# The state space stage of a hybrid decoder step in another order: samples first, one product per batch of log decays, new states on four row groups

## The reference, cut to what matters

```python
    cs = jnp.cumsum(dA, axis=-1)
    Lmat = jnp.exp(segsum(dA))
    CB = jnp.einsum('bclgn,bcsgn->bcgls', Cc, Bc)
    y_diag = jnp.einsum('bcgels,bcsgep->bclgep', CB[:, :, :, None] * Lmat, X)
    decay_states = jnp.exp(cs[..., -1:] - cs).transpose(0, 1, 4, 2, 3)
    states = jnp.einsum('bclgn,bclgep->bcgepn', Bc, X * decay_states[..., None])
    ...
    new_states = jnp.einsum('bgezc,bcgepn->bzgepn', decay_chunk, states)
    y_off = jnp.einsum('bclgn,bcgepn->bclgep', Cc, prev_states) * jnp.exp(cs).transpose(0, 1, 4, 2, 3)[..., None]
    y = (y_diag + y_off).reshape(b, L, H, P)
```

## Time and profile before

| what | value |
|---|---|
| time, median of 3 executions | 1319.71 us (1319.27 to 1320.49) |
| profiled execution: time, span | 1314.85 us, 1313.0 us |
| busy: TensorE, VectorE, ScalarE, GpSimd | 1251.3, 375.7, 229.4, 77.1 us |
| transferred, mean rate | 476.19 MB, 363 GB/s |
| mean granted TensorE clock | 0.984 |

### The profile page before, as it was taken

The page is one execution under the profiler, slowest core; times in us unless marked ns, Lnnn a source line. Parts: engine busy times, 40 slices in busy tenths (PEclk is TensorE's granted clock), DMA queues, the critical chain, the costliest instruction groups (busy, mean ns, idle before and its releaser), DMA issues.

```text
span 1313.0 us, 14836 instructions
## 1 busy us (share of the span) xinstructions
PE 1251.3 (95%) x5826; PEld 541.8 (41%) x5826; DVE 375.7 (29%) x737; ACT 229.4 (17%) x490; POOL 77.1 (6%) x62
## 2 busy tenths in 40 slices
PE   7999998898989999999999999999999999999997
PEld 5766666654433333333333333333333333333332
DVE  2478423543323212122221222212121222212122
ACT  2014434242211111111011011101101111111102
POOL 0000031646000000000000000000000000000000
PEclk9999998899989999999999999999999999999999
DMA  9688779129469999999999999999999999999993
GB/s 276 225 315 276 251 235 347 53 81 324 181 251 426 427 429 429 426 430 429 426 430 427 428 430 426 430 430 426 430 429 427 429 428 428 430 427 428 428 427 132
DMA packets 79581, 476.19 MB, mean 363 GB/s; under 512 B 7688, under 2 KB 41764, under 8 KB 52700
## 3 DMA queue, kind: packets, MB, share of 16 engines
q1 hardware_dynamic: 77278, 471.08, 88.1%
q0 software_dynamic: 688, 2.62, 0.5%
q10 hardware_dynamic: 1582, 2.03, 0.5%
HBM read 468.47 MB, written 7.24 MB: 362 GB/s over the span
## 4 chain that ended last, share of the span: by engine, by line
PE 70%; DMA 23%; DVE 3%; ACT 2%; issue 1%; POOL 1%; SPq 0%; ACTq 0%; DVEq 0%; POOLq 0%
DMA ring<-in_w 23%; PE ps L1991 22%; PE ps L2033 12%; PE ps L1526 9%; PE ps L1940 7%; PE ps L1809 3%; PE ps L1569 1%; PE ps L1948 1%; PE ps L1932 1%; PE ps L1924 1%; PE ps L2009 1%; PE ps L1982 1%; PE ps L1743 1%; PE ps L1545 1%; PE ps L1685 1%
## 5 line engine op out<-in xcount | busy, mean ns | idle before, releaser
L1991 PE MATMUL ps<-ring,own 128*64 128x512 f32 x1536 | 340.9, 593 | 17.1 <-DMA ring<-in_w 17.1
L1450 DVE TENSOR_SCALAR own<-ps 128x512 f32<-128x512 f32 x32 | 22.2, 692 | 649.0 <-PE ps L1991 649.0
L1991 PEld LDWEIGHTS ps<-ring,own 128*64 128x64 f32 x1536 | 108.8, 137 | 236.2 <-issue 197.5
L2033 PE MATMUL ps<-ring,own 128*64 128x512 f32 x768 | 172.7, 599 | 3.4 <-ACT own L953 3.4
L1526 PE MATMUL ps<-own,ring 128*128 128x288 f32 x512 | 131.7, 411 | 0.3 <-DMA ring<-in_w_in 0.3
L1991 PE MATMUL ps<-own 128*64 128x512 f32 x512 | 115.7, 593 | 2.0 <-DMA own<-in_w 2.0
L1526 PEld LDWEIGHTS ps<-own,ring 128*128 128x128 f32 x512 | 95.7, 191 | 30.7 <-issue 3.3
L2033 PEld LDWEIGHTS ps<-ring,own 128*64 128x64 f32 x768 | 54.7, 138 | 107.5 <-issue 104.2
L949 ACT ACTIVATE own<-own 128x512 f32<-128x512 f32 x32 | 20.2, 631 | 443.9 <-DVE own L1450 443.9
L1940 PE MATMUL ps<-own 128*128 128x512 f32 x180 | 90.0, 625 | 0.0
L959 ACT ACTIVATE own<-ps 64x512 f32<-64x512 f32 x64 | 37.9, 593 | 230.0 <-PE ps L2033 229.2
(11 more groups left out here) (337 smaller groups left out, 1051.9 us busy)
## 6 DMA issues: line engine op xcount, KB each, us to landing
ring<-in_w SPq DMA_DIRECT2D x144, 2048.0 KB, 30.6
own<-in_w SPq DMA_DIRECT2D x48, 2048.0 KB, 29.2
ring<-in_w_in SPq DMA_DIRECT2D x16, 1024.0 KB, 6.2
ring<-in_cache_win_k SPq DMA_DIRECT2D x16, 1024.0 KB, 6.8
ring<-in_cache_win_v SPq DMA_DIRECT2D x16, 1024.0 KB, 7.8
ring<-in_w_out SPq DMA_DIRECT2D x6, 1024.0 KB, 10.1
ring<-in_state_ssm SPq DMA_DIRECT2D x8, 512.0 KB, 6.8
out_ssm_sample<-ring SPq DMA_DIRECT2D x8, 512.0 KB, 4.4
```

The source lines that it names most:

```text
L1450: nc.vector.tensor_scalar(xg_o, hid[:, 0], LIMIT, None, ALU.min).then_inc(sem("glu_ready"), 1)
L1991: last = nc.tensor.matmul(ps[C * half:C * half + C, 1 + m, :], xT[:, k, C * u:C * u + C], rows[:, D * half + 512 * m:D * half + 512 * m + ...
L2033: last = nc.tensor.matmul(ps[C * half:C * half + C, 4, :], gT[:, (k % 4) * P + C * (k // 4):(k % 4) * P + C * (k // 4) + C], rows[:, 512 * ...
```

## The change

The stage is rewritten. The samples' rows (tile 2) come first, as one batch of 16 heads x 32 columns; the prompt's eight batches follow (BATCHES). The mask of the decays changes sides, so that a batch of log decays is a single product of 512 columns, in one bank. The old states' transposes and products run at the start of the stage. The new states of a group and of four sequences are one turn of four products with K=32, each on its own 32 partitions; VectorE multiplies the old state by its decay and adds the product in one operation per sequence. X of the samples is laid out as four blocks of rows for this (Xs), B is copied to them (Bn). Old states come in and go out with 512 neighbouring words per row piece in place of 128. Tile 1's square sums, scales and transposes move into the mix. The diff, cut:

```diff
+CHUNK_ORDER = (2, 0, 1)
+CHUNK_TURN = {c: i + 1 for i, c in enumerate(CHUNK_ORDER)}
+BATCHES = [(2, 0)] + [(c, hb) for c in range(2) for hb in range(4)]
+STATE_ON_ACT = (2, 4, 6, 7)
+STATE_ON_DVE = (0, 1, 3, 5)
+ROUNDS = [(0, 0), (1, 0), (0, 1), (1, 1)]
...
+                        sp.dma_start(state[:, b].rearrange("p g j n -> p g (j n)"),
+                                     a["state_ssm"][0, b].rearrange("h p n -> (h p) n").rearrange("(g p j) n -> p g (j n)", g=G, j=4)).then_inc(sem("states_in"), 16)
...
-            sp.wait_ge(sem("yo_ps"), 2)
+            for b in range(DB):
+                if b % 4 == 0:
+                    sp.wait_ge(sem("state_new"), 2 * b + 8)
+                sp.dma_start(o["ssm_sample"][b].rearrange("h p n -> (h p) n").rearrange("(g p j) n -> p g (j n)", g=G, j=4),
+                             state[:, b].rearrange("p g j n -> p g (j n)")).then_inc(sem("ssm_s_out"), 16)
+            sp.wait_ge(sem("M_ready"), len(BATCHES))
...
-                    sp.wait_ge(sem("yo_ps"), 2)
+                    sp.wait_ge(sem("yd_ps"), len(BATCHES))
...
+            decays_in(0)
+            nc.gpsimd.tensor_copy(d3(dAx[0:NS], 16), dA[0:NS, 32:48].unsqueeze(2).broadcast_to([NS, H, 16])).then_inc(sem("dAx_ready"), 1)
             for g in range(G):
                 nc.gpsimd.tensor_tensor(d3(CTm[g], NS), xbcT[:, 10 + g, SEQ:TOK].unsqueeze(1).broadcast_to([P, DB, NS]),
                                         d3(const("seq_cols"), NS), ALU.mult).then_inc(sem("CTm_ready"), 1)
-            pool.wait_ge(sem("fin_out"), 16)
-            nc.gpsimd.tensor_copy(d3(dAx[0:NS], HP), dA[0:NS, 32:48].unsqueeze(2).broadcast_to([NS, H, HP])).then_inc(sem("dAx_ready"), 1)
+            decays_in(1)
+            pool.wait_ge(sem("Bn_ready"), 1)
             for g in range(G):
-                nc.gpsimd.tensor_tensor(Bm[0:NS, g], Bn[0:NS, 2, g * N:(g + 1) * N].unsqueeze(1).broadcast_to([NS, DB, N]),
-                                        const("seq_of", NS).unsqueeze(2).broadcast_to([NS, DB, N]), ALU.mult).then_inc(sem("Bm_ready"), 1)
-
-            pool.wait_ge(sem("decayed_act"), 1)
-            pool.wait_ge(sem("stT_ps"), DB)
-            for j in range(0, 8, 2):
-                nc.gpsimd.tensor_tensor(state[:, :, j, :], state[:, :, j, :], edx[:, 8 * j:8 * j + 8].unsqueeze(2).broadcast_to([P, DB, N]),
-                                        ALU.mult).then_inc(sem("decayed"), 1)
-                if j == 0:
-                    gated(2)
-
-            pool.wait_ge(sem("fs_ps"), 8)
-            pool.wait_ge(sem("yd_out"), 3)
+                nc.gpsimd.tensor_tensor(Bm[:, g], Bn[:, 2, g * N:(g + 1) * N].unsqueeze(1).broadcast_to([P, DB, N]),
+                                        const("seq_of").unsqueeze(2).broadcast_to([P, DB, N]), ALU.mult).then_inc(sem("Bm_ready"), 1)
+            decays_in(2)
+            decayed_x(0)
+            decays_in(3)
+            decays_in(4)
+            gated(2)
+            decays_in(5)
+            pool.wait_ge(sem("yo_ps"), 1)
+            decayed_x(1)
+            decays_in(6)
+            decays_in(7)
+            gated(0)
+            decays_in(8)
+            gated(1)
+
+            pool.wait_ge(sem("st_ps"), 2)
...
+            chunk_decays(2)
+            chunk_decays(0)
+            act.wait_ge(sem("decay_ps"), 1)
+            nc.scalar.activation(edx, ps[:, 7, 256:272], ACT.Exp).then_inc(sem("decayed_act"), 1)
+            decay_weights(0)
+            state_columns(2)
+            state_columns(4)
+            decay_weights(1)
+            state_columns(6)
+            decay_weights(2)
+            state_columns(7)
+            decay_weights(3)
+            decay_weights(4)
+            chunk_sums(2)
+            chunk_decays(1)
+            for batch in range(5, 9):
+                decay_weights(batch)
+            chunk_sums(0)
+            act.wait_ge(sem("y_sums"), 4)
+            nc.scalar.activation(dts[:, 6:9], stat[:, 6:9], ACT.Sqrt)
+            for c in (0, 2):
+                n = ROWS[c]
+                last = nc.scalar.activation(dts[0:n, 2 * c:2 * c + 2], stat[0:n, 2 * c:2 * c + 2], ACT.Sqrt, bias=stat[0:n, 60:61])
+            last.then_inc(sem("mix_rt"), 1)
+            act.wait_ge(sem("fin_ps"), 1)
+            nc.scalar.activation(d3(fin_nat, 512), ps[:, 6:8, :], ACT.Copy).then_inc(sem("fin_ready"), 1)
...
+            def new_states(turn):
+
+                g, half = ROUNDS[turn]
+                dve.wait_ge(sem("decayed_act"), 1)
+                dve.wait_ge(sem("fs_ps"), turn + 1)
+                for b in range(4 * half, 4 * half + 4):
+                    nc.vector.scalar_tensor_tensor(state[:, b, g], state[:, b, g], edx[:, 8 * g + b:8 * g + b + 1], ps[:, 4:8, N * (b % 4):N * (b % 4) + N],
+                                                   ALU.mult, ALU.add).then_inc(sem("state_new"), 1)
...
+            chunk_start(2)
+            chunk_start(0)
+            state_columns(0)
+            state_columns(1)
+            weights(0)
+            sample_x()
+            state_columns(3)
+            sample_diagonal()
+            state_columns(5)
+            weights(1)
+            weights(2)
+            sample_carried()
+            new_states(0)
+            weights(3)
+            new_states(1)
+            weights(4)
+            new_states(2)
+            chunk_start(1)
+            new_states(3)
+            add_diagonal(0)
+            weights(5)
+            dve.wait_ge(sem("st_ps"), 1)
+            nc.vector.tensor_copy(St, both(6)).then_inc(sem("St_ready"), 1)
+            weights(6)
+            add_carried()
+            weights(7)
+            dve.wait_ge(sem("st_ps"), 2)
+            link(nc.vector.tensor_tensor(d3(St, HP), d3(St, HP), ex[1][:, 32:48].unsqueeze(2).broadcast_to([P, H, HP]), ALU.mult))
+            nc.vector.tensor_tensor(St, St, both(2), ALU.add).then_inc(sem("St_ready"), 1)
+            weights(8)
+            add_diagonal(1)
...
-                for u in range(4):
-                    last = nc.tensor.matmul(ps[0:n, 2 + batch % 2, u * P:u * P + n], d3(dAm[batch % 2], P)[0:n, u, 0:n], le(batch // 4), start=True, stop=True)
-                last.then_inc(sem("seg_ps"), 1)
+                c, _ = BATCHES[batch]
+                n = ROWS[c]
+                pe.wait_ge(sem("leA_ready"), batch + 1)
+                if batch:
+                    pe.wait_ge(sem("L_ready"), batch)
+                else:
+                    pe.wait_ge(sem("cs_ready"), 1)
+                nc.tensor.matmul(ps[0:n, 1, :], gt(c), leA[batch % 2][0:n], start=True, stop=True).then_inc(sem("seg_ps"), 1)
...
+                g, half = ROUNDS[turn]
+                if turn:
+                    pe.wait_ge(sem("state_new"), 4 * turn)
+                for j in range(4):
+                    last = nc.tensor.matmul(ps[:, 4 + j, :], Xs[NS * j:NS * j + NS, g, :],
+                                            Bm[NS * j:NS * j + NS, g, 4 * half:4 * half + 4, :].rearrange("p b n -> p (b n)"), start=True, stop=True)
+                last.then_inc(sem("fs_ps"), 1)
...
+            gram(2)
+            gram(0)
+            pe.wait_ge(sem("states_in"), 16 * DB)
+            old_state(0)
+            pe.wait_ge(sem("dAx_ready"), 1)
+            for g in range(G):
+                last = nc.tensor.matmul(ps[:, 7, 256 + 8 * g:264 + 8 * g], dAx[0:NS, P * g:P * g + P], const("seq_of", NS), start=True, stop=True)
+                if g == 0:
+                    last.then_inc(sem("expert_slot_used"), MIX_BASE - 1)
+            last.then_inc(sem("decay_ps"), 1)
+            log_decays(0)
+            old_state(1)
+            pe.wait_ge(sem("CTm_ready"), 2)
+            old_outputs(0)
+            old_state(2)
+            old_outputs(1)
+            diagonal(0)
+            old_state(3)
+            old_outputs(2)
+            old_state(4)
+            old_outputs(3)
+            log_decays(1)
+            old_state(5)
+            old_outputs(4)
+            old_state(6)
+            old_outputs(5)
+            log_decays(2)
+            old_state(7)
+            old_outputs(6)
+            old_outputs(7)
+            gram(1)
+            pe.wait_ge(sem("Xs_ready"), 1)
             pe.wait_ge(sem("Bm_ready"), 2)
-            pe.wait_ge(sem("Xd_ready"), 3)
+            pe.wait_ge(sem("yd_out"), 1)
+            new_states(0)
+            diagonal(1)
+            log_decays(3)
+            new_states(1)
+            diagonal(2)
+            log_decays(4)
+            new_states(2)
+            diagonal(3)
+            new_states(3)
+            diagonal(4)
+            log_decays(5)
+            pe.wait_ge(sem("state_new"), 16)
+            chunk_state(0)
+            log_decays(6)
+            pe.wait_ge(sem("St_ready"), 1)
+            for g in range(G):
+                last = nc.tensor.matmul(ps[:, 6 + g, :], xbcT[:, 10 + g, cols(1)], St[:, 512 * g:512 * g + 512], start=True, stop=True)
+            last.then_inc(sem("yo_ps"), 1)
+            diagonal(5)
```

(27 more changed lines are left out.)

355 lines of the change are left out of this document (146 added, 209 removed).

## The result

The changed kernel takes 1308.37 us (median of 5 runs, 1307.67 to 1311.13), the kernel before 1319.71 us (5 runs, 1315.08 to 1322.13). The ratio is 0.9922, 95% interval 0.9899 to 0.9945: about 10 us faster. The mean of the three, 0.9933, is 8.8 us. The profiled execution has a span of 1306.5 us, 6.5 less than before.

A forecast was written before the change was run, and what follows sets the result against it. The expert weight stream was taken as the bound, its start set by when TensorE reaches the experts. Stage steps put the first w_out product at 294.2, 10.6 us earlier: 1304.25, plus 4.9 to the median, 1309.1 us; range 1302.3 to 1318.5.

The forecast's parts named there:

- a round: New states in the stage: one group of four products, four fused operations and two hand-overs, 4.05 us; four rounds follow.
- the relay: Step of the stage after the rounds: the prompt's carried state passed between two engines, 15.4 us, to 284.5.
- serial: Rival for the new states: row groups run one after the other, 3.5 us a group, 1318.5 us; chance 0.08.
- dear fused operation: Rival for the new states: a fused operation takes 1.2 us, sixteen cost 8 more, 1317.1 us; chance 0.07.
- the clock stays low: Rival: TensorE granted 1.2 GHz from 251 to the mix, first w_out product at 310.3, 1325.2 us; chance 0.08.
- merged log decays: Four products per batch of 128 columns become one of 512: from 1.1 to 0.89 us a batch at full clock.
- Step (b): Early stage, TensorE in its own order: transposes, old-state products, samples' diagonal, two log decays; to 250.2 us.
- Step (f): A second half-clock stretch of 18 us assumed in the stage, costing 5.2 us; first w_out product at 294.2.
- the carried part: Before the four rounds, VectorE adds the carried part: 2 x 0.7 + 1.2 = 2.6 us.
- a block that moves as a whole: From the first w_out product (304.81 us) to the experts (380 us), TensorE nearly always at work, so counted as shifting together.
- a loss of 3 to 6 us behind the stage: Rival: part of the gain lost to late b1 rows or late w_out, about 1313.5 us; chance 0.1.
- slack of 3.7 us: Behind the stage, between memset L720's start at 324.99 and VectorE's need after 328.66; expected to shrink to about 1.

The follow-up runs named there:

- x_one_group: Changed kernel with all four products of a turn of new states on one row group; 1333.89 us, ratio 1.0113 to the kernel before.
- x_unfused: Changed kernel with each of the sixteen fused state operations split into decay and addition; 1323.12 us, ratio 1.0033 to the kernel before.
- x_sums_later: Changed kernel with square sums behind the samples' diagonal, subtraction reading PSUM, routing table cleared before the last b1 rows; 1304.99 us, 0.9887 of the kernel before.
- x_free_start: Changed kernel with square sums and Bn copies behind the first state columns, subtraction reading PSUM; 1313.0 us, ratio 0.9940 to the kernel before.
- x_sums_late: Changed kernel with only the square sums behind the first state columns, subtraction reading PSUM; 1312.17 us, ratio 0.9932 to the kernel before.
- x_four: Changed kernel with each batch's log decays as four products of 128 columns instead of one of 512; 1308.76 us, ratio 0.9906 to the kernel before.
- c_after: The changed kernel run again, unchanged, as reference for other runs; 1311.28 us, ratio 0.9946 to the kernel before.

## Why the prediction was right, point by point

**Right: the experts bound the time.** The ninth unit is issued at 376.72 and the last lands at 1272.35, 895.6 us (895.8 predicted), and the column "to end" moves by 1.2 us over fourteen profiles. Whatever the stage gains or loses up to the first expert product arrives whole at the end; x_one_group and x_unfused show it for losses, x_sums_later for a gain.

**Right: the prices in the stage.** Row groups 1.14 us (1.15 taken), fused operation 0.68 (0.7), a round 4.05 at full clock (4.05), four rounds 16.8 us from 256.47 to 273.29 (16.2), the relay 14.5 us from 273.29 to 287.8 (15.4). The Trainium skill's 3.07 times for four row groups ("TensorE: Matmul & The Clock Gate", "Why this matters for your kernels") would make 1.15 us of the 3.5 us estimated for a series, an estimate too. The trace agrees: in x_one_group a series takes 7.19 us at half clock, 3.6 at full clock by halving (an estimate), which is 3.2 times 1.14. Changes of tiling mode show no price in these rows. The rivals "serial", "dear fused operation" and "the clock stays low" fall. The merged log decays are the one price that was wrong, 0.02 us a batch instead of 0.2.

**Right in the sum, by errors that cancel.** Step (b) put the end of the old outputs at 250.2; it came at 253.64, 3.4 us late. I had let VectorE wait for GpSimd 0.3 us a batch of weights and looked nowhere else. The trace shows 2.82 us of idle TensorE at the very start, and with it a half-clock stretch that lasts until 238 instead of 231.45. Step (f) then counted 5.2 us for a second low stretch of 18 us (three rounds at 2.05 us more would even be 6.1). The clock fell once between 250 and 275, as expected, but for 4 us in the second round only (4.63 us instead of 4.05), and it fell again for 7 us around the mix transposes, which the prediction had named as a sign of being wrong. Together: 3.4 us late before the rounds, 4.6 early by the short stretch, 0.9 early in the relay, and 1.0 late in the carried part (2.8 instead of 2.6) and between the relay and the mix (5.3 instead of 4.5) give 293.1 against 294.2. That the sum is within 1.1 us is luck as much as skill. x_sums_later removes the first error's cause, and its stage is 2.1 us shorter than the shortest of the changed kernel's.

**Wrong: "a block that moves as a whole".** Between the first w_out product and the first expert product the changed kernel takes 79.4 to 80.4 us where the kernel before took 75.7. TensorE's own rows tell where the 4.2 us of the first profile went. The changed kernel's first three products with w_out (six records), then five of the kernel before (ten records) behind its first router products:

```profile
293.10 4.12 PE L1913 MATMUL ps<-ring,own 128*128 128x512 f32 x6
```

```profile
340.06 6.17 PE L1809 MATMUL ps<-ring,own 128*128 128x512 f32 x10
```

The first six records take 4.12 us instead of 2.81, since the half-clock stretch of 289 to 296 reaches into them: 1.3 us. The pause for GpSimd is 1.52 us instead of 0.63: 0.9 us. In the stretch of 330 to 337 lie eight small transposes (1.01 us instead of 0.72) and the ten records that follow (7.51 us instead of 6.17): 1.6 us. The remaining 0.4 us come later. So some 3 of the 4.2 us are the clock and 0.9 is GpSimd.

The rival that named a loss of 3 to 6 us behind the stage (0.1) was therefore true in its size and partly in its place: the b1 rows did land late. The prediction had them ahead by 8 us. They were asked for 9.7 us earlier (290.26 instead of 299.94), but GpSimd could start on them only 1.5 us earlier:

```profile
308.89 1.89 POOL L708 CAST own<-ring 96x2048 bf16<-96x2048 f32 x1 [7.35 <-DMA ring<-in_b]
```

```profile
307.41 1.89 POOL L715 CAST own<-ring 96x2048 bf16<-96x2048 f32 x1 [15.43 <-DMA ring<-in_b]
```

The first is the kernel before. What the prediction took for a slack of 3.7 us was in truth 8 (the table was clear at 325.8, and VectorE could go on only at 333.88, behind TensorE's sample products), which is why 10 us of lost lead cost so little directly. Over the thirteen profiles of changed kernels, the eight with a short stretch after the pause, or none, take 76.5 to 77.3; the five with a long one take 78.3 to 80.4. That is a correlation over profiles, and the pause for GpSimd goes with it; what lengthens the stretch stays open.

**Right in the end, with luck.** 1309.1 us was forecast and 1308.37 measured. But like with like, the forecast was 4 us too low: it gave 1304.25 us for the profiled execution, by 10.6 us off the one of the kernel before, and that execution took 1308.37, 6.5 us less. This is what the lost 4.2 us behind the stage and the last microsecond make of 11.7. What closed the gap was the step of 4.9 us between the kernel before's profiled execution and its median, which the prediction added and which the changed kernel's first five runs don't have (their profiled execution is their median). Two of the three measurements of this kernel give 0.9946 and 0.9932, 7 to 9 us faster. The half-clock stretch at 172 us, in some executions and not in others, is of the size of that step.

## What to carry to other kernels

- Before summing a stage's steps, find the point whose time alone sets the end, and check in several profiles that the distance from it to the end is constant. Then every edit can be judged in the trace by when that point comes, far below the noise of the time.
- A VectorE operation on SBUF can last as long as the GpSimd operations beside it (0.16 us became 1.53, 0.69 became 5.57). Read from PSUM where that is possible, and put the others where nothing that TensorE wants is queued behind them; moving them elsewhere only moves the hold (x_free_start, x_sums_late).
- A cost in a stage where TensorE pauses can be paid twice, once in its own microseconds and once in clock: 13 us for sixteen extra operations whose own work is some 6, 22 us for row groups in series that by themselves cost some 10.
- A wait that has just become the last one is worth only the part by which it is last (0.9 of 5.4 us here). To say that a run acquits it, check that the wait is still there in that run: x_four and x_free_start were no such runs.

## What the runs showed of the hardware that was not expected

VectorE held by GpSimd: a subtraction of 0.16 us takes 1.53, a square sum of 0.69 takes 5.57 through four GpSimd operations in a row, a scaling of 0.48 takes 4.28. Operations with a PSUM source beside them keep their time (0.41 us for L1210 at 232.22, 0.68 us for each fused operation at 270.52). The Trainium skill ("SBUF — State Buffer", "SBUF: two separate sides") has this as a port pair that is locked for a whole instruction by whichever of the two engines comes first, for VectorE's operations in a two-port mode, or with two SBUF inputs where the GpSimd operation reads SBUF too; the traces agree, and add that VectorE can lose the lock several times in a row (5.57 us).

The half-clock stretches differ between executions of one and the same kernel, in a place where the rows count TensorE as fully busy in both (172 us in c_after, not in the first profile; before it 47 products of 16 columns in both), and move the start of the stage by some 4 us.

A fused operation (scale, then add) of 128 x 512 f32 with one operand in four banks of PSUM takes 0.68 us, as long as one with both tensors in SBUF (0.69 us, L1453 in the earlier trace rows).
